# A float32 two-block transformer kernel: activation combinations and one weight sum move from VectorE to GpSimd, and a copied product becomes the start of another one in PSUM

## The reference

```python
h = layer_norm(DN_ALPHA * h + 0.5 * swiglu(h, ffn_w_in[i, 0], ffn_w_out[i, 0]), ln_g[i, 0], ln_b[i, 0])
# swiglu: silu(h @ w_gate) * (h @ w_up) @ w_out, hidden width 2816 = 11 steps of 256
```

## Time and profile before

| | |
|---|---|
| median of 3 runs | 1524.89 us |
| the profiled execution: time / span | 1523.43 us / 1521.5 us |
| TensorE busy | 98% of the span |
| VectorE busy / ScalarE busy / GpSimd busy | 73% / 55% / 10% |
| mean granted TensorE clock | 0.994 |

### The profile page before, as it was taken

One profiled execution on the slowest core, in us unless ns is written; L12 is line 12 of the kernel. 1 busy time (PEld: TensorE's weight loads), 2 busy tenths in 40 slices (PEclk: granted clock), 3 DMA queues, 4 the chain that ended last, 5 costly groups with the idle time before them and its releaser, 6 DMA issues.

```text
span 1521.5 us, 18598 instructions
## 1 busy us (share of the span) xinstructions
PE 1490.0 (98%) x7654; PEld 1258.1 (83%) x7654; DVE 1112.7 (73%) x1135; ACT 833.1 (55%) x839; POOL 156.4 (10%) x152
## 2 busy tenths in 40 slices
PE   8899999989999999999999989999999999999997
PEld 6688888878888788888888868888898888888886
DVE  5887687787877977787567787867686556785555
ACT  5656467565565665554434556555636566354443
POOL 0400020110002000024021200002002200020000
PEclk9999999999999999999999999999999999999999
DMA  9777454477837777555544677746444434465551
GB/s 356 268 231 229 182 204 169 150 262 277 295 106 296 218 241 256 166 227 188 179 160 169 224 249 226 269 163 237 154 167 142 164 139 166 166 222 194 193 191 58
DMA packets 46595, 310.08 MB, mean 204 GB/s; under 512 B 5568, under 2 KB 6016, under 8 KB 10800
## 3 DMA queue, kind: packets, MB, share of 16 engines
q1 hardware_dynamic: 38592, 270.35, 47.8%
q0 software_dynamic: 6112, 34.80, 9.9%
q10 hardware_dynamic: 1808, 3.74, 0.6%
HBM read 282.60 MB, written 1.05 MB: 186 GB/s over the span
## 4 chain that ended last, share of the span: by engine, by line
PE 83%; DVE 7%; DMA 6%; issue 1%; ACT 1%; POOL 1%; SPq 0%; POOLq 0%; DVEq 0%; ACTq 0%
PE psum L1988 16%; PE psum L1992 15%; PE psum L1991 15%; PE psum L2097 7%; PE psum L2124 6%; PE psum L2101 4%; DVE weights_lo L1174 4%; DMA weights_raw_more<-weights_raw_more 3%; PE psum L2240 3%; PE psum L2237 3%; PE psum L2236 3%; PE psum L2131 3%; DMA weights_raw_more<-in_weights 2%; PE psum L2020 1%; PE psum L2033 1%
## 5 line engine op out<-in xcount | busy, mean ns | idle before, releaser
L1174 DVE TENSOR_TENSOR weights_lo<-weights_raw,weights_hi 128x2048 fp32r<-128x2048 f32 x191 | 440.9, 2312 | 198.0 <-ACT weights_hi L609 196.6
L609 ACT ACTIVATE weights_hi<-weights_raw 128x2048 fp32r<-128x2048 f32 (+1 forms) x198 | 372.4, 1883 | 194.9 <-PE psum L1992 136.2
L1174 DVE TENSOR_TENSOR weights_lo<-weights_raw_more,weights_hi 128x2048 fp32r<-128x2048 f32 x56 | 128.2, 2289 | 70.5 <-ACT weights_hi L609 70.5
L1988 PE MATMUL psum<-weights_hi,hidden_hi 128*128 128x512 f32 x416 | 163.9, 394 | 3.3 <-DVE weights_lo L1174 3.3
L1991 PE MATMUL psum<-weights_lo,hidden_hi 128*128 128x512 f32 x416 | 162.4, 390 | 0.0
L1992 PE MATMUL psum<-weights_hi,hidden_lo 128*128 128x512 f32 x416 | 162.1, 390 | 0.0
L1988 PE MATMUL psum<-weights_hi,operand 128*128 128x512 f32 x384 | 151.5, 394 | 0.0
L1991 PE MATMUL psum<-weights_lo,operand 128*128 128x512 f32 x384 | 149.8, 390 | 0.0
L609 ACT ACTIVATE weights_hi<-weights_raw_more 128x2048 fp32r<-128x2048 f32 x56 | 107.1, 1913 | 70.1 <-DMA weights_raw_more<-weights_raw_more 39.2
L1992 PE MATMUL psum<-weights_hi,operand 128*128 128x512 f32 x352 | 137.2, 390 | 0.0
L2097 PE MATMUL psum<-operand,weights_hi 128*128 128x512 f32 x544 | 129.4, 390 | 0.0
(11 more groups left out here) (386 smaller groups left out, 2799.9 us busy)
## 6 DMA issues: line engine op xcount, KB each, us to landing
weights_raw<-in_weights SPq DMA_DIRECT2D x198, 1024.0 KB, 4.8
weights_raw_more<-in_weights SPq DMA_DIRECT2D x56, 1024.0 KB, 8.9
weights_raw_more<-weights_raw_more POOLq DMA_DIRECT2D x20, 1024.0 KB, 7.2
ln_rows<-in_ln_rows POOLq DMA_DIRECT2D x16, 512.0 KB, 7.3
weights_raw_more<-weights_raw POOLq DMA_DIRECT2D x4, 1024.0 KB, 12.3
weights_raw<-in_weights SPq DMA_DIRECT2D x4, 256.0 KB, 4.3
weights_raw<-in_weights SPq DMA_DIRECT2D x2, 512.0 KB, 6.7
normalised<-in_x POOLq DMA_DIRECT2D x2, 512.0 KB, 11.1
```

The costliest lines, as they stand in the source:

```text
L609: nc.scalar.activation(hi[:, rest], whole[:, rest], ACT.Copy).then_inc(hi_split, 1)
L1174: nc.vector.tensor_tensor(lo_of(n), raw_of(n), hi_of(n).bitcast(F32), ALU.subtract).then_inc(lo_split, 1)
L1988: mm(out, a_hi, b_hi, start=start, stop=False, skip_group_check=True)
```

## The change

1. The five sums of the activation forms and the four remainders (nine operations of 128 x 512) move from VectorE to GpSimd, as new function `first_forms`; the order of the forms is 0, 3, 2, 1.
2. `t3` (128 x 2048, one for each group, 12 in all) moves from VectorE to GpSimd, between `t1`'s and `t4`'s transfers on its queue.
3. `t1` of the first group of each feed-forward part is no longer a transfer but a VectorE addition (4 in all).
4. Step 1 is computed with `features_unit` (three matmuls of 256 columns for each block) in place of `features_both` (one of 512 and one of 256); ScalarE's two copies and VectorE's two sums for it go away.
5. Product 1 is copied by ScalarE into the PSUM bank of product 3, which accumulates on it; TensorE therefore waits for that copy before product 3, and VectorE's addition (L1373) goes. The copy waits for the hidden units of the step before. The next combination is written to PSUM instead of `squares`.

```diff
-SUMMED = FFN_STEPS - 2 - 2 * len(GROUPS)
+SUMMED = FFN_STEPS - 3 - 2 * len(GROUPS)
+FORM_ORDER, FORM_SUMS = (0, 3, 2, 1), (1, 5, 4, 2)
...
+            def first_forms(f):
+
+                if f:
+                    pool.wait_ge(x_kept, 4 * f)
+                else:
+                    pool.wait_ge(x_lo_done, KC // 2)
+                x11, x12, x21, x22 = x_part(0, 0), x_part(0, 1), x_part(1, 0), x_part(1, 1)
+                nc.gpsimd.tensor_tensor(x22, x22, x21, ALU.subtract).then_inc(form_summed, 1)
+                nc.gpsimd.tensor_tensor(x21, x11, x21, ALU.subtract).then_inc(form_summed, 1)
+                pool.wait_ge(form_summed, 5 * f + 1)
+                nc.gpsimd.tensor_tensor(x11, x22, x11, ALU.add).then_inc(form_summed, 1)
+                pool.wait_ge(form_summed, 5 * f + 3)
+                nc.gpsimd.tensor_tensor(x12, x11, x12, ALU.subtract).then_inc(form_summed, 1)
+                pool.wait_ge(form_summed, 5 * f + 4)
+                nc.gpsimd.tensor_scalar(x11, x11, -1.0, 0.0, ALU.mult, ALU.add).then_inc(form_summed, 1)
+                for at, k in enumerate(FORM_ORDER):
+                    pool.wait_ge(form_hi_done, 4 * f + at + 1)
+                    nc.gpsimd.tensor_tensor(by_chunk(form_lo(k)), in_form[k], by_chunk(form_hi(k)).bitcast(F32),
+                                            ALU.subtract).then_inc(form_ready, 1)
+
+            def add_t3(n0, f, s):
+
+                n = n0 + GROUP_AT[s]
+                t2, t3 = raw_of(n + 1), raw_of(n + 5)
+                pool.wait_ge(lo_split, n + 1)
+                pool.wait_ge(tile_added, tile_sums(f, s) + 1)
+                nc.gpsimd.tensor_tensor(t3, t2, t3, ALU.subtract).then_inc(t3_added, 1)
...
+                first_forms(f)
                 for s in GROUPS:
                     if s != GROUPS[0]:
                         add_t1(n0, f, s)
+                    add_t3(n0, f, s)
                     add_t4(n0, f, s)
...
-                    split_hi(n + 3, (tile_added, 2 * g + 1))
-                    copy_back(n + 1, p1, 0)
+                    if s > 2:
+                        split_hi(n + 3, (tile_added, tile_sums(f, s) + 1))
+                    act.wait_ge(hid_done, j0 + s)
+                    copy_back(n + 1, work[:, 2, :], 0)
+                    if s == 2:
+                        split_hi(n + 3, (tile_added, tile_sums(f, s) + 1))
...
-                    split_hi(n + 5, (tile_added, 2 * g + 2))
+                    split_hi(n + 5, (t3_added, g + 1))
...
-                features_both(n0 + 2, unit_banks(1), between=lambda: turn_hidden(j0, 2 * P, acc[:, 3:4, :]), second_free=kept)
+                features_unit(n0 + 2, pairs[1], between={4: turn_first})
...
-                    product(n + 2, 2, block_of_x(0, 1), True)
                     pe.wait_ge(copied_back, 3 * g + 1)
+                    product(n + 2, 2, block_of_x(0, 1), False)
```

More of the change, by code:

```diff
@@ L375, in build @@
         group_index = lambda f, s: len(GROUPS) * f + GROUPS.index(s)
+        dma_sums = lambda f, s: (len(GROUPS) - 1) * f + GROUPS.index(s)
+        tile_sums = lambda f, s: (len(GROUPS) + 1) * f + GROUPS.index(s) + 1
         against_hi, against_lo = (lambda t: t[:, :, 0:TOK]), (lambda t: t[:, :, TOK:2 * TOK])
-        summed_before = lambda f, j: SUMMED * f + sum(1 for s in range(1, j) if s not in GROUPS and s - 1 not in GROUPS)
+        summed_before = lambda f, j: SUMMED * f + sum(1 for s in range(2, j) if s not in GROUPS and s - 1 not in GROUPS)
         gate_of = lambda j: pairs[1] if j == 1 else pairs[0]
@@ L685, in forms_hi @@
                 def forms_hi():
-                    for k in range(4):
-                        act.wait_ge(form_summed, 4 * f + k + 1)
+                    for k in FORM_ORDER:
+                        act.wait_ge(form_summed, 5 * f + FORM_SUMS[k])
                         nc.scalar.activation(by_chunk(form_hi(k)), in_form[k], ACT.Copy).then_inc(form_hi_done, 1)
@@ L747, in ffn @@
                 hidden_hi(j0, 0, two(acc[:, 3, :]))
-                summed_step(1, n0 + 4, 2)
+                act.wait_ge(weights_used, n0 + 4)
+                nc.scalar.activation(silu_g[:, :, :], two(pairs[1][:, 0, :]), ACT.Silu).then_inc(silu_done, 1)
+                split_hi(n0 + 6)
+                act.wait_ge(hid_done, j0 + 2)
+                hidden_hi(j0 + 1, 1, hid[:, 0:2, :])
                 units = ffn_units()
@@ L1313, in last_step @@
                     hidden_lo(j0 + j, j % 3, hid[:, 0:2, :])
[L1315 to L1335, removed]
                 def loaded(load):
@@ L1363, in group, with less @@
                     g = group_index(f, s)
-                    t1, t3 = raw_of(n + 1), raw_of(n + 5)
                     up = slice(TOK, 2 * TOK)
[L1367 to L1373, removed]
-                    def less(out, b, used, copied):
+                    def less(out, kept, b, used, copied):
                         dve.wait_ge(copied_back, 3 * g + copied)
                         dve.wait_ge(weights_used, used)
-                        nc.vector.scalar_tensor_tensor(out=out, in0=work[:, b, :], scalar=-1.0, in1=out, op0=ALU.mult,
+                        nc.vector.scalar_tensor_tensor(out=out, in0=work[:, b, :], scalar=-1.0, in1=kept, op0=ALU.mult,
                                                        op1=ALU.subtract).then_inc(combined, 1)
                     split_lo(n + 3)
-                    add_t3()
                     split_lo(n + 4)
@@ L1385, in group @@
                     split_lo(n + 6)
-                    first_block()
-                    less(p6, 1, n + 5, 3)
-                    less(p5[:, :], 0, n + 6, 2)
+                    less(work[:, 3, :], p6, 1, n + 5, 3)
+                    less(p5[:, :], p5[:, :], 0, n + 6, 2)
                     split_lo(n + 7)
                     dve.wait_ge(group_silu, 3 * g + 1)
-                    nc.vector.tensor_tensor(hid[:, 0:2, :], silu_g[:, :, :], p1_p6[:, :, up], ALU.mult)
+                    nc.vector.tensor_tensor(hid[:, 0:2, :], silu_g[:, :, :], work[:, 2:4, up], ALU.mult)
                     split_lo(n + 8)
@@ L1403, in ffn @@
                 split_lo(n0 + 3)
-                form_sums()
                 hidden(j0, pairs[0][:, :, TOK:2 * TOK])
+                add_t1(2)
                 split_lo(n0 + 4)
-                forms_lo()
                 split_lo(n0 + 5)
                 hidden_lo(j0, 0, two(acc[:, 3, :]))
-                summed_step(1, 2)
+                add_t2(2)
+                dve.wait_ge(hid_ready, j0 + 1)
+                hidden(j0 + 1, two(pairs[1][:, 1, :]))
+                split_lo(n0 + 6)
+                hidden_lo(j0 + 1, 1, hid[:, 0:2, :])
                 units = ffn_units()
@@ L2218, in ffn, with turn_first @@
                 unit_banks = lambda j: (gate_of(j), up_of(j))
[L2219 to L2220 removed]
+                def turn_first():
+                    if f:
+                        pe.wait_ge(x_kept, 4 * f)
+                    turn_hidden(j0, 2 * P, acc[:, 3:4, :])
+                features_unit(n0 + 2, pairs[1], between={4: turn_first})
                 def next_down(j, n, hooks={}):
                     pe.wait_ge(hid_ready, j0 + j + 1)
[L2225 to L2226 removed]
+                    if j == 0 and f:
+                        pe.wait_ge(x_kept, 4 * f)
                     at = 2 * (j % 3)
```

34 lines of the change are left out of this document (17 added, 17 removed).

## The result

The changed kernel takes 1528.22 us (median of 10 runs, 1526.46 to 1530.73) against 1524.7 us of ten runs of the kernel before beside it (1523.22 to 1526.0): ratio 1.0024, 95% interval 1.0015 to 1.0033. It is slower by 0.24%, 3.5 us; 1541 had been forecast, with a range of 1528 to 1558, so the result stands at the range's lowest edge. The profiled execution took 1530.73 us, the longest of its ten, at a span of 1528.9 us and a mean granted clock of 0.989; before it was 0.994.

The account below looks back on a forecast made before the run. TensorE, busy 1490.0 of 1521.5 us, was taken as the bound. First groups 5, other groups 8 and clock 3 made +16 us on the profiled 1523.43, 1.5 under the median: 1541 on the median, range 1528 to 1558.

Parts of the forecast that it names:

- the lock: GpSimd and VectorE exclude each other at their shared SBUF ports; an operation waits for the whole of the other one.
- the end where turns are taken: First groups, GpSimd gets in at the next VectorE boundary: tile 2 to tile 10 sums to 146.0 against 144.4, +1.6 us.
- the other: First groups, GpSimd gets in only where VectorE is idle: tile 2 to tile 10 sums to 154.1 us, +9.7.
- +5 between them: First groups: +5 us taken between the ends of +1.6 and +9.7, since GpSimd got in at two of five boundaries.
- the clock's 3: Half-clock spells behind each first group's stall above 2.5 us: 3 us in all, range 0 to 7.
- The other groups (8): Eight later groups: t3 on GpSimd loses 0.3 to 2.7 us each; 1 taken, 8 us in all (2 to 22).
- The change without contention: First groups if GpSimd's work held nothing up: tile 2 to tile 10 sums to 114.6 against 144.4, 29.8 us gained.
- stretch of 28.2 us: Tile 2 to tile 10 without gaps in the second to fourth part, said to include 0.4 us for the dearer step 1.
- Product 3's wait for the copy of product 1 costs nothing then: First groups without contention: ScalarE has 2.72 us, product 2, for a copy of some 0.6 us.
- Rival (a): The lock matters little: up to 29.8 us gained, 1495 us, or 1510 with half of it; chance 22%.
- (b): GpSimd starved at every boundary: +9.7, 8 times 2.7 and the late t1s, 1560 to 1568 us; chance 8%.
- (c): Balance: stalls only move, 1522 to 1528 us; chance 6%.

Follow-up runs that it names:

- b1: a1 with t3 of the eight later groups on GpSimd; 1507.69 us, ratio to the kernel before 0.9888.
- b2: b1 with those t3 let in only after the remainder of the group's fifth tile, four VectorE operations later; 1530.52 us, ratio to the kernel before 1.0040.
- a1: The changed kernel with all form operations and t3 back on VectorE; 1507.14 us, ratio to the kernel before 0.9890.
- c1: The kernel before plus parts 3 and 4 of the change; 1502.36 us, ratio to the kernel before 0.9859.
- c2: The kernel before plus parts 3 and 5 of the change; 1509.71 us, ratio to the kernel before 0.9907.
- b3: a1 plus 3 GpSimd operations of t3's size that nobody waits for, in the second to fourth part; 1515.51 us, ratio to the kernel before 0.9942.
- b4: a1 plus 27 GpSimd operations of the forms' size that nobody waits for, in the second to fourth part; 1527.27 us, ratio to the kernel before 1.0020.
- a4: The kernel before plus part 3 of the change alone; 1506.82 us, ratio to the kernel before 0.9889.
- a3: The changed kernel with the forms' sums and remainders back on VectorE, t3 on GpSimd; 1518.48 us, ratio to the kernel before 0.9962.

## Why the prediction was right or wrong

**Right: what bounds, and the lock.** The sign, the place of the stalls, `t3`'s length (4.6 forecast, 4.57 measured), remainders of 3 to 7 us, the gap before tile 6 behind L747 (some 3 us forecast; 3.82, 3.49 and 3.49 in the later parts, 0.52 in the first), and the wait at a low part behind VectorE. The latter came one tile early, at tile 6 and not at tile 7, since `t3` went in ahead of tile 6's remainder. One sign was wrong: `t3` was to be recorded at 5 to 9 us, and all twelve took 4.56 to 4.95. It never waited for more than the end of one short VectorE operation.

**Right in the sum, by luck: the first groups.** Tile 2 to tile 10 in the order of the parts: 38.6, 36.0, 35.7, 35.7 forecast at the end where turns are taken, 39.8, 38.3, 38.0, 38.0 at the other, before the clock; measured 38.3, 38.6, 35.6, 37.4 with the clock in it. Terms of 5 us for the stalls and 3 for the clock stand against 5.5 measured for both. The windows part them roughly. In the second part the clock is low until 341.1, and behind 334.92 no further wait stands before tile 10, so these 6.2 us at half clock cost 3.1. In the same way it is 2.2 us in the fourth part (903.32 to 907.7) and 1.7 in the first (from 43.88 on for 3.4 us), and nothing in the third, where a wait of 1.45 us follows. That is an estimate of 7.0 us where 3 was put, and it leaves 36.6, 35.5, 35.6 and 35.2 for the stalls: the end where turns are taken, or 3.1 us less in all. So "+5 between them" was too much, the clock's 3 too little, and the two errors offset each other.

**Wrong: "The other groups (8) ... I take 1 us, 8 us in all (2 to 22)".** This term was mis-sized. Both its ends were worked out well: 0.3 at one, measured 0.07 (b1); 2.7 at the other, measured 2.85 (b2). The value between them had no case behind it. `t3` is issued right behind `t2`, VectorE's next operation there is the short one of the hidden units, and where turns are taken GpSimd is in at once, so that end holds in all eight. In the changed kernel 1.9 us were lost outside the first groups, most of it once, at 95.12 in the first part; at the same place of the second part the same hold of 6.71 us cost nothing.

**The rest of the miss.** On profiled executions, 1539.4 was forecast and 1530.7 measured: 8.7 us, of which 6.1 are the later groups (8 less 1.9) and 2.5 the first ones with the clock (8 less 5.5). The other 4.0 lie between one profiled execution and the median: 2.5 by which the changed kernel's was above it, and the 1.5 that I had added. So the mechanism was right and three terms were mis-sized, the later groups most.

**Half wrong: "The change without contention ... 29.8 us gained".** a1 keeps the forms and `t3` on VectorE and gains 17, c1 gains 21; a version in which they cost nothing on either side wasn't built, so the 29.8 stays unshown. Its stretch of 28.2 us is 17.3 + 10.9, without the 0.4 for step 1 that it names beside it. (The chances of "slower" add up to 0.74 and not to 0.72.) "Product 3's wait for the copy of product 1 costs nothing then" holds only if the hidden units of step 1 are in time: with the sums on VectorE it costs 2.9 us (c2). That step 1 gets dearer was seen, that it frees VectorE by more than it costs TensorE was in the sum without contention but never priced by itself. Part 3's 17 us were hidden in the same sum, where nobody could see that one edit carried most of the gain.

**Rival (a)** fell: GpSimd's work costs 21.1 us, and the stretches lost 5.5 us rather than gain. **(b)** fell with the trace, where `t3` got in at once in all twelve groups, and with b1. **(c)**, "stalls only move", named 1522 to 1528 us for it, and its words describe the result well: idle time 32.2 against 31.5 us. But the balance is one of a gain of some 17 us by parts 3 to 5 and a loss of 21 by parts 1 and 2, not of nothing with nothing.

## What to carry to other kernels

Price each edit of a bundle by itself: here one of five gave 17 us and two others took 21, and the sum looked like no change. Before work moves to an engine that shares its access to SBUF with VectorE, look for the stretch where VectorE's list has no pause. There each hold reaches TensorE: 2.8 us for one operation (b3). In the later groups the same `t3` held VectorE just as long (6.71 us for one remainder) and cost 0.07 us, since TensorE had work until VectorE had caught up. Let in four VectorE operations later it cost 2.85 again (b2), because its result was late. So ask both what the moved work holds up and when its result is wanted. Where two ends of an unknown are far apart, find the row that decides between them instead of a value in the middle.

## What the runs showed of the hardware

- Between two busy lists VectorE and GpSimd took turns, one operation each, at all the boundaries of the forms in b4 that the rows show, although VectorE never paused. The Trainium skill (SBUF — State Buffer, section "SBUF: two separate sides") has the pair of ports as an exclusive lock for a whole instruction; b3 and b4 agree, with 2.29 against 5.38 us and 0.69 against 1.53.
- Turns aren't the whole rule. The residual of 8.99 us in the trace before, which stood through three boundaries, comes again in a4 at the same place (8.97 us; both operations, then all of L485, min/median/max in ns). VectorE's boundaries at 41.95, 44.15 and 46.35 passed before it got in at 48.6. It has one input where those of b4 have two; whether that decides wasn't tried.

```profile
40.59 12.02 POOL L485 TENSOR_SCALAR residual<-normalised 128x1024 f32<-128x1024 f32 x2
...
L485 POOL TENSOR_SCALAR residual<-normalised x16: 1047/3077/8967, 40.6 to 1326.1; 128x1024 f32<-128x1024 f32 x16
```

- An addition of 128x2048 on GpSimd took 4.60 us with two different inputs (b2, with VectorE idle) and 3.60 with the same input twice (b3). Why wasn't tried.
- In the second part TensorE's clock fell to its lower level of 1.2 GHz behind stalls of 2.54 (before), 3.82 (after) and 2.04 us (b3), for 3.4, 10.2 and 3.4 us. Behind 1.37 us (a4) it did not fall, nor behind 3.04 (a3), nor behind 2.04 in the third part of b3. So the length of the stall alone doesn't decide; what does stays open. Windows of a3 behind its stall, then of b3:

```profile
326.00:345.00 19.00, 15.90 (x69) 12.40 (x68) 19.00 (x11) 11.36 (x10) 2.24 (x2) 1.00 0.72 216
...
327.90:331.30 3.40, 3.40 (x9) 2.67 (x8) 3.40 (x3) 0.00 (x0) 0.00 (x0) 0.51 0.93 193
```
